# Order of the recurrent stage's gate and query tiles in a two-block kernel

## What is computed

```
h = rms_norm(x, norm_g) * (1.0 + scale) + shift
proj = h @ w_in
(hq, hf, hi, hz, rq, rk, rv, rz, ga, gb) = jnp.split(proj, offsets, axis=-1)
# recurrence (HGRN2), 8 heads of 128:
q = silu(hq)
f = lb + (1.0 - lb) * sigmoid(hf)
k = 1.0 - f;  logf = log(f)        # then cumulative sums of logf, chunk by chunk
```

## Time and profile before

| what | value |
|---|---|
| median of three runs | 2723.68 us (2721.24 to 2726.33) |
| profiled execution | 2722.56 us |
| its span | 2720.5 us |
| TensorE busy | 2612.7 us (96%) |
| VectorE busy | 1667.6 us (61%) |
| GpSimd busy | 1132.4 us (42%) |
| ScalarE busy | 842.5 us (31%) |
| granted TensorE clock, mean | 0.987 of full |

### The profile page before, as it was taken

How to read it: one execution, slowest core, us unless ns; L and a number is a source line. 1 busy time by engine, 2 the same in 40 slices (tenths; PEclk the granted TensorE clock), 3 DMA queues, 4 the chain that set the end, 5 groups by cost and what they waited for, 6 DMA issues and landing times.

```text
span 2720.5 us, 33162 instructions
## 1 busy us (share of the span) xinstructions
PE 2612.7 (96%) x13218; PEld 2180.7 (80%) x13218; DVE 1667.6 (61%) x2208; ACT 842.5 (31%) x1326; POOL 1132.4 (42%) x651
## 2 busy tenths in 40 slices
PE   6999888989999999999999999999999999999998
PEld 5788777877788877888888887788888888888887
DVE  4879967767513488666674468804355465476566
ACT  4011233324323333333332436212222222343342
POOL 2433000036630638777764443664222322242364
PEclk8999999999999999999999999999999999999999
DMA  4122233235311412222245553573333342465682
GB/s 150 62 86 94 96 121 125 82 98 201 124 63 62 155 65 77 86 78 90 77 143 190 160 185 122 180 258 106 124 109 109 126 138 100 154 257 210 216 309 109
DMA packets 147381, 360.25 MB, mean 132 GB/s; under 512 B 15173, under 2 KB 51229, under 8 KB 147100
## 3 DMA queue, kind: packets, MB, share of 16 engines
q1 hardware_dynamic: 65072, 177.81, 20.1%
q10 hardware_dynamic: 82156, 180.33, 18.5%
HBM read 268.90 MB, written 89.19 MB: 132 GB/s over the span
## 4 chain that ended last, share of the span: by engine, by line
PE 83%; DVE 9%; ACT 2%; POOL 2%; issue 2%; DMA 2%; ACTq 1%; DVEq 0%; POOLq 0%
PE pp L295 31%; PE pp L2172 13%; PE pp L2225 9%; PE pp L277 8%; PE pp L493 6%; PE pp L2902 2%; PE pp L1250 2%; POOL w_lo L3601 1%; DVE hgin_b L2708 1%; PE pp L1936 1%; PE pp L1915 1%; POOL w_hi L3599 1%; PE pp L1563 1%; PE pp L2922 1%; PE pp L2923 1%
## 5 line engine op out<-in xcount | busy, mean ns | idle before, releaser
L3599 POOL CAST w_hi<-w_raw 128x1024 fp32r<-128x1024 f32 x184 | 218.9, 1190 | 1017.4 <-PE pp L295 691.4
L295 PE MATMUL pp<-w_hi,act_hi 128*128 128x512 f32 x1344 | 541.3, 403 | 11.9 <-POOL w_lo L3601 7.8
L295 PE MATMUL pp<-w_hi,act_lo 128*128 128x512 f32 x1344 | 528.3, 393 | 0.0
L295 PE MATMUL pp<-w_lo,act_hi 128*128 128x512 f32 x1344 | 526.0, 391 | 0.0
L3601 POOL TENSOR_TENSOR w_lo<-w_raw,w_hi 128x1024 fp32r<-128x1024 f32 x184 | 470.2, 2556 | 14.7
L295 PEld LDWEIGHTS pp<-w_hi,act_hi 128*128 128x128 f32 x1344 | 253.8, 189 | 67.4 <-POOL w_lo L3601 9.1
L295 PEld LDWEIGHTS pp<-w_hi,act_lo 128*128 128x128 f32 x1344 | 253.4, 189 | 58.2
L295 PEld LDWEIGHTS pp<-w_lo,act_hi 128*128 128x128 f32 x1344 | 253.8, 189 | 51.2
L493 PE MATMUL pp<-act_hi,w_hi 128*128 128x512 f32 x480 | 191.8, 400 | 15.4 <-DVE act_lo L830 6.5
L2143 POOL TENSOR_TENSOR w_lo<-w_raw,w_hi 128x1024 fp32r<-128x1024 f32 x52 | 133.7, 2573 | 164.0 <-ACT w_hi L2137 163.9
L493 PE MATMUL pp<-act_lo,w_hi 128*128 128x512 f32 x480 | 189.5, 395 | 0.0
(11 more groups left out here) (468 smaller groups left out, 5307.7 us busy)
## 6 DMA issues: line engine op xcount, KB each, us to landing
w_raw<-in_weights SPq DMA_DIRECT2D x314, 512.0 KB, 3.5
z_s<-hg_st ACTq DMA_DIRECT2D x52, 512.0 KB, 3.8
hid_s<-ffn_cb ACTq DMA_DIRECT2D x22, 512.0 KB, 2.6
ffn_graw<-hid_s ACTq DMA_DIRECT2D x44, 256.0 KB, 3.1
hg_qkb<-hT_s SPq DMA_DIRECT2D x16, 512.0 KB, 8.2
qkvT_s<-mixin_o ACTq DMA_DIRECT2D x12, 512.0 KB, 2.8
gdn_qkv<-qkvT_s ACTq DMA_DIRECT2D x8, 768.0 KB, 5.1
front_x<-in_x ACTq DMA_DIRECT2D x8, 512.0 KB, 5.2
```

What stands on the lines that cost most here:

```text
L295: last = pe.matmul(dst, a[:, k, t * P:(t + 1) * P], columns(w, j, k, 0, n), start=(k == 0 and a is high and w is w_hi), stop=(k == NK - 1 ...
L3599: pool.tensor_copy(hi, raw).then_inc(w_split, 1)
```

## The change

The order of the tiles becomes: queries of the first token half, gates of the first half, gates of the second half, queries of the second half. The weight stream follows (query strips, gate strips twice, query strips). The transposes of the last four token tiles stand after the fourth, fifth, sixth and seventh tile. On ScalarE the first eight silus take the place of the first sigmoids, with the four `high` steps and four weight casts between them; the four sigmoids follow. The constants' loads move from after the fourth silu to after the eleventh, and the loads of the recurrence's chunks from after the silus 11 and 13 to after 13 and 14. On VectorE the `low` steps of tiles 4 to 7 come after all four `normalise` steps.

```diff
             def pe(self, pe):
                 R = self.prev.norm
-                for j in range(2 * self.JOBS):
-                    h, m = j // NK % 2, j % NK
-                    strip = FIRST_STRIP["hf_hq"] + j // 2
-                    if j < self.JOBS and m == 0:
+                for at in range(2 * self.JOBS):
+                    h, m = int(at >= 2 * NK), at % NK
+                    strip = FIRST_STRIP["hf_hq"] + at // 2
+                    if at in (0, 2 * NK):
                         R.ready(pe, h)
                     weights_ready(pe, strip)
-                    if 4 <= j < self.JOBS + 4:
-                        after(pe, self.sigs, "sig", j - 4)
-                    elif j >= self.JOBS + 4:
-                        after(pe, self.qs, "q", j - 4 - self.JOBS)
+                    if NK + 4 <= at < NK + self.JOBS + 4:
+                        after(pe, self.sigs, "sig", at - 4 - NK)
+                    elif at >= 4:
+                        after(pe, self.qs, "q", at - 4 if at < NK + 4 else at - 4 - self.JOBS)
...
-                    for t in {1: (4,), 2: (5,), 3: (6, 7)}.get(j, ()):
-                        R.turn(pe, t)
+                    if 3 <= at < 7:
+                        R.turn(pe, at + 1)
 
             def act(self, act):
...
-                R.second(act, 5)
-                sig(0)
-                R.high(act, 4)
-                R.second(act, 6)
-                sig(1)
-                R.high(act, 5)
-                R.second(act, 7)
-                self.prev.cast_down(act, N_DOWN * 2 + 4)
-                self.prev.cast_down(act, N_DOWN * 2 + 5)
-                sig(2)
-                R.high(act, 6)
-                R.high(act, 7)
-                sig(3)
-                self.prev.cast_down(act, N_DOWN * 2 + 6)
-                self.prev.cast_down(act, N_DOWN * 2 + 7)
...
+                R.second(act, 5)
+                silu(0)
+                R.second(act, 6)
+                silu(1)
+                R.second(act, 7)
+                self.prev.cast_down(act, N_DOWN * 2 + 4)
+                self.prev.cast_down(act, N_DOWN * 2 + 5)
+                silu(2)
+                silu(3)
+                R.high(act, 4)
+                self.prev.cast_down(act, N_DOWN * 2 + 6)
+                self.prev.cast_down(act, N_DOWN * 2 + 7)
+                for j in range(4, NK):
+                    silu(j)
+                    if j < NK - 1:
+                        R.high(act, j + 1)
+                for j in range(4):
+                    sig(j)
...
-                        silu(0)
-                        silu(1)
+                        silu(NK)
+                        silu(NK + 1)
...
-                for j in range(2, self.JOBS):
+                for j in range(NK + 2, self.JOBS):
                     silu(j)
-                    if j == 3:
+                    if j == NK + 2:
                         for t, name in LATE:
                             act.dma_start(full(t), d[name]).then_inc(late_loaded, 16)
-                    if j == NK + 2:
+                    if j == NK + 4:
                         self.kept(act)
                         self.queries(act, NK)
                         self.scan.load(act, 0)
-                    if j == NK + 4:
+                    if j == NK + 5:
                         self.scan.load(act, 1)
 
             def dve(self, dve):
...
                 R.normalise(dve, 5)
-                R.low(dve, 4)
                 R.scale(dve, 7)
                 R.normalise(dve, 6)
-                R.low(dve, 5)
                 R.normalise(dve, 7)
-                R.low(dve, 6)
-                R.low(dve, 7)
+                for t in range(NT // 2, NT):
+                    R.low(dve, t)
...
-    for c0 in (hf, hf, hq, hq):
+    for c0 in (hq, hf, hf, hq):
         out += [*strips(w_in2, int(c0), D // SC)]
```

More of the change, by code:

```diff
@@ L2591, in pe @@
                 R = self.prev.norm
-                for j in range(2 * self.JOBS):
-                    h, m = j // NK % 2, j % NK
-                    strip = FIRST_STRIP["hf_hq"] + j // 2
-                    if j < self.JOBS and m == 0:
+                for at in range(2 * self.JOBS):
+                    h, m = int(at >= 2 * NK), at % NK
+                    strip = FIRST_STRIP["hf_hq"] + at // 2
+                    if at in (0, 2 * NK):
                         R.ready(pe, h)
                     weights_ready(pe, strip)
-                    if 4 <= j < self.JOBS + 4:
-                        after(pe, self.sigs, "sig", j - 4)
-                    elif j >= self.JOBS + 4:
-                        after(pe, self.qs, "q", j - 4 - self.JOBS)
-                    self.made.done(product_half(pe, strip, m % 2, bank(2 * (j % 4)), h, frees=(m % 2 == 0)), "tile")
-                    if j == 1:
+                    if NK + 4 <= at < NK + self.JOBS + 4:
+                        after(pe, self.sigs, "sig", at - 4 - NK)
+                    elif at >= 4:
+                        after(pe, self.qs, "q", at - 4 if at < NK + 4 else at - 4 - self.JOBS)
+                    self.made.done(product_half(pe, strip, m % 2, bank(2 * (at % 4)), h, frees=(m % 2 == 0)), "tile")
+                    if at == 1:
                         self.prev.released(pe)
-                    for t in {1: (4,), 2: (5,), 3: (6, 7)}.get(j, ()):
-                        R.turn(pe, t)
+                    if 3 <= at < 7:
+                        R.turn(pe, at + 1)
             def act(self, act):
@@ L2612, in sig @@
                     s = j % 4
-                    after(act, self.made, "tile", j)
+                    after(act, self.made, "tile", j + NK)
                     prior(act, V, "k", j - 4)
@@ L2619, in store @@
                     act.dma_start(hT_s[dst, m * P:(m + 1) * P, h * 512:(h + 1) * 512], src[j % 4][:, :]).then_inc(done[j % 4], 16)
-                R.second(act, 5)
-                sig(0)
-                R.high(act, 4)
-                R.second(act, 6)
-                sig(1)
-                R.high(act, 5)
-                R.second(act, 7)
-                self.prev.cast_down(act, N_DOWN * 2 + 4)
-                self.prev.cast_down(act, N_DOWN * 2 + 5)
-                sig(2)
-                R.high(act, 6)
-                R.high(act, 7)
-                sig(3)
-                self.prev.cast_down(act, N_DOWN * 2 + 6)
-                self.prev.cast_down(act, N_DOWN * 2 + 7)
                 def silu(j):
-                    after(act, self.made, "tile", j + self.JOBS)
+                    after(act, self.made, "tile", j if j < NK else j + self.JOBS)
                     act.wait_ge(self.qst[j % 4], 16 * (j // 4))
```

## The result

The kernel after the change takes 2738.69 us (median of 7 runs, 2728.55 to 2744.61), the kernel before, timed beside it, 2725.55 (7 runs, 2720.55 to 2733.59). The ratio is 1.0041, with a 95% interval of 1.0023 to 1.0058: slower by 0.4%, some 11 us. I had forecast +1.1 us and a range up to 2731.5, so the result lies outside it.

The account below looks back on a forecast made before the run. TensorE, busy 96% of the span, was taken as the bound, so only its pauses could change. Terms -0.4 + 1.0 + 0.2 + 0.3 = +1.1 us gave 2723.7 (2724.8 on the median), range 2718 to 2731.5.

Parts of the forecast that it names:

- the last term: At the next stage's start: the last silu, behind the second scan load's issues, wanted 2.7 us in, costs +0.3 us.
- 0.3 + 1.0 + 0.2: Around the next stage's start: late last silu +0.3, later weight halves +1.0, risk of late VectorE scan work +0.2 us.
- Rival (b): Crowded stage end: ScalarE's stores and loads beside the next weights pause TensorE 3 to 4 us; +6.5, 2730 us; chance 0.23.
- Its two conditions: At the crowded end: a weight half takes 7.4 us, or the first scan load lands after 1847.
- (b)'s bound: At the crowded end: 7.4 us weight halves, fourth split 29.4 after tile 29's start, or first scan load landing after 1847.
- Tile 5: Fifth tile in TensorE's queue: starts at 1676.7 after one 4.5 us pause, waiting for POOL's weight split.
- The slow clock behind it: After the pause at tile 5: TensorE loses 2.2 us to the lower clock, bounds 1.7 and 3.4.
- the rule that I cited: TensorE clock: an idle TensorE falls to the lower clock and stays there a while; the change pays 1.7 us at least.
- First logarithm: On ScalarE, after tile 12 and four sigmoids: comes at 1727.2, with VectorE idle until then.
- The gate chain: VectorE, ScalarE and store issues, first logarithm to ninth query's silu: 88.6 us, slower than TensorE, which waits at tile 29.
- The 1.0 that I took off for the first scan: First group of four gates: first scan no longer behind a slowed VectorE operation, an estimated gain of 1.0 us.
- the exclusion that I had cited: VectorE and GpSimd exclude each other for whole instructions; one VectorE operation takes 0.43 us mostly, 2.6 beside a split.

Follow-up runs that it names:

- e1: The changed kernel with both scan loads issued on ScalarE's queue after the last silu; ratio to the kernel before 1.0015 (1.0003 to 1.0027).
- f4: The changed kernel with tile 5's casts early, constants' loads between the first sigmoids and second scan load behind the last silu; ratio to before 0.9986 (0.9969 to 1.0003).
- f3: The changed kernel with the two casts for tile 5's weights moved ahead of the second silu; ratio to before 1.0004 (0.9988 to 1.0020).
- e4: The changed kernel's tile order, with transposes, high and low parts back where they were before; ratio to before 1.0023 (1.0009 to 1.0036).
- f2: The kernel before, old tile order, with constants' and scan loads moved as late as in the change; ratio to before 1.0002 (0.9985 to 1.0019).
- e2: The changed kernel with the eight constant loads issued between the first four sigmoids; ratio to before 1.0015 (1.0003 to 1.0028).
- g1: The changed kernel with the constants' loads issued by SyncE's queue at about the same time; ratio to before 1.0040 (1.0025 to 1.0054).

## Why the prediction was wrong, step by step

**The failed step** is the last term: "The last silu, behind the second scan load's issues, is wanted 2.7 into the next stage: +0.3." I saw the place, the order and the due time, and even the start of the scan loads (183.4 after the stage's start forecast, 182.9 measured). But 0.3 leaves room only for issues as long as before, 2.36 and 2.84 us for three. In the crowd that I had myself counted (445 GB/s wanted), they took 7.27 and 5.31. The wait was 8.02, and with the slow clock behind it and the rest the stretch cost 9.1 instead of 0.3 + 1.0 + 0.2. I had allowed for transfers that come late, not for their issues holding the engine.

**Rival (b)** had the place and named the order on ScalarE's queue, but let it act through transfers that land late, and its price was +6.5 against 10.9. Its two conditions weren't met: a weight half took 5.7 in the median, not 7.4. The weights came later than I took, but less than it needed: the fourth half was split 28.4 after tile 29's start (26.4 before, 29.4 at (b)'s bound). POOL's row for this, then VectorE's first of the recurrence, answering to the earlier trace rows:

```profile
1851.03 2.34 POOL L3601 TENSOR_TENSOR w_lo<-w_raw,w_hi 128x1024 fp32r<-128x1024 f32 x1
```

```profile
1853.97 0.48 DVE L2959 MEMSET hg_both<- 128x512 f32 x1 [29.78 <-DMA hg_qkb<-hT_s]
```

TensorE would have wanted the half at 1846.81 + 4.1, so 2.5 of lateness lay under the silu's wait; e1 (1.92) and f4 (2.40) laid it bare. The first load landed 7.2 into the next stage, with (b)'s bound at 9.3; its VectorE work was covered, as I said.

**Tile 5: right.** Forecast at 27.1 after the start, behind an unbroken pause of 4.5 ended by POOL; it was 27.14 and 4.34. TensorE's row names no releaser, but POOL's split ended 0.10 ahead of it (1678.07, 6.00 long). The slow clock behind it: forecast 2.2, measured 1.4 up to tile 9 (53.05 - 27.14 - 4 x 5.45 - 3 x 0.9), with a window mean of 0.93. That was a cheap draw: the six kernels with this pause took 7.68 to 9.24 for tile 5 and its transposes, 6.35 in f3 at full clock, so 1.3 to 2.9 over. The Trainium skill ("TensorE: Matmul & The Clock Gate", "Part 1: The HAM clock gate") adds to the rule that I cited that the slow start differs between runs of one kernel. No run here shows two profiles of one kernel; between kernels the traces agree. Tile 5 took 5.52 in e4 and 7.17 in before after nearly the same pauses. And nine kernels had a pause of 2.0 ahead of one gate tile: in after (at 1778.55, granted clock 0.76 over the next 7 us) and in f2 that tile took 7.2, in the other seven 5.5 to 5.6.

**First logarithm: right** (76.9, forecast 77.6). ScalarE's rows of the chain, first logarithm of each group and first silu, answering to the earlier trace rows:

```profile
1733.95 0.63 ACT L2649 ACTIVATE hgin_l<-hgin_f 128x512 f32<-128x512 f32 x1
...
1759.92 0.63 ACT L2649 ACTIVATE hgin_l<-hgin_f 128x512 f32<-128x512 f32 x1
...
1806.24 0.63 ACT L2649 ACTIVATE hgin_l<-hgin_f 128x512 f32<-128x512 f32 x1
...
1824.19 0.60 ACT L2624 ACTIVATE hgin_q<-pp 128x512 f32<-128x512 f32 x1
```

**The gate chain: right in kind, 2.4 too short.** 91.0 from the first logarithm to tile 29, against 88.6 (and 91.4 to 91.6 in the kernels with the same pause). The first group took 25.97, where I had 23.6 less 1.0; the later two took 23.5 and 22.8. The 1.0 that I took off for the first scan was no gain, since the slowing only moved from one operation to the next. The scans of the first eight gates and of the second eight, after and then before (line, operation, count: ns min/median/max, first and last start), answering to the earlier trace rows:

```profile
L2708 DVE TENSOR_TENSOR_SCAN hgin_b<-hgin_keep,hgin_l x8: 1223/1789/3231, 1734.6 to 1776.5; 128x512 f32<-128x512 f32 x8
...
L2708 DVE TENSOR_TENSOR_SCAN hgin_b<-hgin_keep,hgin_carry,hgin_l x8: 1272/1284/3293, 1784.1 to 1822.9; 128x512 f32<-128x512 f32 x8
```

```profile
L2708 DVE TENSOR_TENSOR_SCAN hgin_b<-hgin_keep,hgin_l x8: 1214/1225/1920, 1686.1 to 1723.4; 128x512 f32<-128x512 f32 x8
...
L2708 DVE TENSOR_TENSOR_SCAN hgin_b<-hgin_keep,hgin_carry,hgin_l x8: 1284/2179/3509, 1731.4 to 1770.7; 128x512 f32<-128x512 f32 x8
```

A scan takes 1.2 to 1.3 us by itself and up to 3.2 to 3.5 when a split of POOL runs beside it: the exclusion that I had cited. The medians say only which operation the splits happen to meet: the first eight scans were slower than before, the second eight faster. Only the first group was dearer, 3.9 more than before's 22.0, where I had given it 1.6; the second and third together took 0.9 less than before's 24.1 and 23.1. Tile 29 came at 167.90, forecast 166.3, and the stage's end at +1.3 instead of -0.4. The pause of some 1 us that I had put at tile 25 did not come, and that at tile 29 was 0.96 and not some 2: TensorE had already waited 2.02 at tile 21 and run slowly behind it, where I had put nothing.

**Part 1 as a whole: right as a loss.** I had put the later transposes at 0.6 of level and 0.5 of clock; against e4, after and e2 are 2.1 and 3.7 later at tile 9, and 1.4 and 3.5 at the stage's end.

## What to carry to other kernels

An issue of a DMA holds its engine, and for how long depends on what the DMA engines still have to do: one of 512 KB here took 0.8 us in the quiet stretch and 2.4 in the crowd. Before moving transfers next to each other, ask what compute instruction stands behind their issues on the same queue and who waits for it; keep loads that nobody needs soon behind the last instruction that another engine waits for. And where a move brings several stages' traffic together, price the issues at the crowded rate, not from rows of the quiet stretch.

## What the runs showed of the hardware that I had not expected

**Length of issues.** Three issues of 512 KB each on ScalarE, with the DMA share and rate while they were issued:

| kernel, burst | three issues, us | DMA share | GB/s |
|---|---|---|---|
| before, first and second | 2.36 and 2.84 | 0.70 and 0.82 | 181 and 211 |
| after, first and second | 7.27 and 5.31 | 1.07 and 1.11 | 381 and 342 |
| e2, first and second | 3.42 and 6.87 | 1.04 and 1.05 | 351 and 345 |
| f2, first and second | 2.55 and 6.30 | 0.74 and 1.11 | 200 and 335 |
| f4, first and second | 3.33 and 3.52 | 1.00 and 0.93 | 335 and 231 |
| g1, first and second | 6.62 and 4.16 | 1.06 and 1.14 | 380 and 318 |

Up to a share of 0.82 they are short. From 0.93 they are 3.3 to 7.3, and e2's first burst and g1's differ twofold at the same share, so the share does not set the length: the 1.6 MB still outstanding on another queue do. What it is that fills up stays open.

**One pause or two.** One unbroken pause of 4.3 to 4.7 us cost TensorE 1.3 to 2.9 us of slow clock within the next tile; two pauses of 2.2 to 2.4 and 1.2 with 1.1 of transposes between them cost 0.1 (e4) and 1.7 (before). A single pause of 2.0 cost 1.6 in two kernels and nothing in seven.

**The start of the stage.** The stage's start, with nothing changed ahead of it, lies between 1647.7 and 1659.7 in the twelve profiles, so single profiles here can't be compared by their ends.
